# A planner that lets the parts of a dense matmul row follow each other with no latency between them

## What is computed

```python
h = rms_norm(x, norm_mix);  proj = h @ w_in               # block 0, in-projection 1024 -> 3352
o_nsa  = nsa_mixer(q, kc, vc, ks, vs, kw, vw, gates)      # 8 heads of 64
o_hgrn = hgrn2_mixer(hq, hf, hi, hg, lower_bounds, gain)  # 4 heads of 128
x = x + concat(o_nsa, o_hgrn) @ w_out
h = rms_norm(x, norm_ffn)
x = x + (silu(h @ w_gate) * (h @ w_up)) @ w_down
for l in range(2):                                        # blocks 1 and 2
    sb_q, sb_k, sb_v, df_q, df_k, df_v = split(rmsnorm(x, attn_norm[l]) @ w_in_2[l])
    mixed = concat(stick_breaking(sb_q, sb_k, sb_v), rmsnorm(differential(rope(df_q), rope(df_k), df_v)))
    x = x + mixed @ w_o[l]
    x = x + square(relu(rmsnorm(x, mlp_norm[l]) @ w_ff1[l])) @ w_ff2[l]
return rmsnorm(x, final_norm)
```

## Time and profile before

| | us |
|---|---|
| median of three timed executions | 1883.1 (1882.93 to 1883.12) |
| the profiled execution | 1884.4 |
| its span, first to last instruction | 1882.7 |
| PE busy | 1849.6 (98% of the span) |
| DVE busy | 1331.4 (71%) |
| ACT busy | 924.6 (49%) |
| POOL busy | 306.6 (16%) |

### The profile page before, as it was taken

One profiled execution on the slowest core, in us unless ns is written; L12 is line 12 of the kernel. 1 busy time (PEld: TensorE's weight loads), 2 busy tenths in 40 slices (PEclk: granted clock), 3 DMA queues, 4 the chain that ended last, 5 costly groups with the idle time before them and its releaser, 6 DMA issues.

```text
span 1882.7 us, 25125 instructions
## 1 busy us (share of the span) xinstructions
PE 1849.6 (98%) x9460; PEld 1547.3 (82%) x9460; DVE 1331.4 (71%) x2096; ACT 924.6 (49%) x1572; POOL 306.6 (16%) x378
## 2 busy tenths in 40 slices
PE   9999999999999999999999999999999999999998
PEld 7888778888888887878888888888878788888886
DVE  5476778555557877679965568787758976557886
ACT  4445776332224654457642236554547753225663
POOL 3133354000000000002412220000002322221000
PEclk9999999999999999999999999999999999999999
DMA  7222110288886662222247765563221227765664
GB/s 246 57 59 96 57 46 23 91 301 271 264 291 216 193 191 79 90 68 61 64 159 278 236 236 175 180 213 114 78 90 46 68 95 260 246 227 197 208 192 141
DMA packets 140151, 291.81 MB, mean 155 GB/s; under 512 B 12640, under 2 KB 53632, under 8 KB 140032
## 3 DMA queue, kind: packets, MB, share of 16 engines
q1 hardware_dynamic: 140032, 290.23, 46.9%
HBM read 243.00 MB, written 47.19 MB: 154 GB/s over the span
## 4 chain that ended last, share of the span: by engine, by line
PE 83%; DVE 7%; ACT 5%; POOL 2%; issue 2%; DMA 0%; POOLq 0%; SPq 0%; DVEq 0%; ACTq 0%
PE ps L49 80%; PE ps L52 3%; DVE wlo L71 2%; ACT sk1h L65 1%; POOL p L71 1%; ACT whi L65 1%; ACT p L62 1%; DVE hTl L71 1%; DVE htmp L79 1%; ACT L62 1%; DVE p L91 1%; DVE x L71 1%; ACT htmp L62 1%; POOL hTl L71 1%; DVE rot L71 0%
## 5 line engine op out<-in xcount | busy, mean ns | idle before, releaser
L65 ACT ACTIVATE whi<-raw 128x1024 fp32r<-128x1024 f32 (+1 forms) x359 | 376.0, 1051 | 480.7 <-PE ps L49 474.5
L71 DVE TENSOR_TENSOR wlo<-raw,whi 128x1024 fp32r<-128x1024 f32 (+1 forms) x359 | 442.6, 1235 | 218.4 <-ACT whi L65 214.8
L49 PE MATMUL ps<-hTh,whi 128*128 128x512 f32 (+1 forms) x1176 | 442.7, 376 | 0.0
L49 PE MATMUL ps<-hTh,wlo 128*128 128x512 f32 (+1 forms) x1176 | 438.1, 373 | 0.0
L49 PE MATMUL ps<-hTl,whi 128*128 128x512 f32 (+1 forms) x1176 | 437.9, 372 | 0.0
L49 PE MATMUL ps<-whi,hTh 128*128 128x512 f32 x934 | 374.8, 401 | 6.0 <-DVE hTl L71 3.8
L49 PE MATMUL ps<-whi,hTl 128*128 128x512 f32 x934 | 365.6, 391 | 0.0
L49 PE MATMUL ps<-wlo,hTh 128*128 128x512 f32 x934 | 365.2, 391 | 0.0
L49 PEld LDWEIGHTS ps<-hTh,wlo 128*128 128x128 f32 x1176 | 221.0, 188 | 39.5
L49 PEld LDWEIGHTS ps<-hTh,whi 128*128 128x128 f32 x1176 | 221.2, 188 | 37.0 <-DVE wlo L71 0.4
L49 PEld LDWEIGHTS ps<-hTl,whi 128*128 128x128 f32 x1176 | 221.3, 188 | 36.4
(11 more groups left out here) (260 smaller groups left out, 2470.7 us busy)
## 6 DMA issues: line engine op xcount, KB each, us to landing
raw<-in_w_ff_dram SPq DMA_DIRECT2D x96, 512.0 KB, 4.4
raw<-wsum_dram SPq DMA_DIRECT2D x64, 512.0 KB, 4.1
raw<-in_w_gate_up_dram SPq DMA_DIRECT2D x88, 256.0 KB, 4.1
wsum_dram<-htmp SPq DMA_DIRECT2D x44, 512.0 KB, 4.7
wsum_dram<-u SPq DMA_DIRECT2D x42, 512.0 KB, 5.7
raw<-in_w_in_dram SPq DMA_DIRECT2D x40, 512.0 KB, 4.6
raw<-in_w_in_dram SPq DMA_DIRECT2D x68, 256.0 KB, 3.1
u<-in_w_ff_dram SPq DMA_DIRECT2D x32, 512.0 KB, 6.1
```

The lines of the kernel that those rows point to most:

```text
L49: return self.eng.matmul(out, l, r, start=start, stop=stop, skip_group_check=True)
L65: return self.eng.activation(out, in_, ACT.Copy)
L71: return self.eng.tensor_tensor(out, a, b, op)
```

## The change

`Plan.add` notes, for a step of the sequences `gemm`, `gemm_up` and `op`, which step is before it in its sequence; `Plan.run` lets that step follow at the end of the one before, without the 0.2. Users in other sequences and on other engines still get the latency. Nothing else is changed: the same instructions are issued, with the same waits, and their order in the queues is whatever the planner now gives.

```diff
+CLOSE = ("gemm", "gemm_up", "op")
+
+
 class Plan:
     def __init__(self, T):
-        self.T, self.steps, self.rings, self.last = T, {}, {}, {}
+        self.T, self.steps, self.rings, self.last, self.behind = T, {}, {}, {}, {}
...
         if seq is not None:
             after = after + ((self.last[seq],) if seq in self.last else ())
+            self.behind[key] = self.last.get(seq) if seq in CLOSE else None
             self.last[seq] = key
...
             for u in users.get(key, ()):
                 waiting[u][0] -= 1
-                waiting[u][1] = max(waiting[u][1], end[key])
+                waiting[u][1] = max(waiting[u][1], t + dur if self.behind.get(u) == key else end[key])
```

## The result

The changed kernel takes 1889.05 us (median of six executions, 1886.9 to 1891.37) against 1883.11 for the kernel before: a ratio of 1.0027, with a 95% interval of 1.0018 to 1.0037. It is slower by some 6 us where I had forecast 4.8 us less. The profiled execution took 1890.9 us, its span is 1889.0.

A forecast was written before the change was run, and what follows sets the result against it. The bound was PE's work in sequence plus about 21 us of mixer waits. Terms: -1.9 - 1.3 - 3.2 + 1.6 = -4.8 us, so 1884.4 became 1879.6, less 1.3: 1878.3 us; 8-in-10 range 1869 to 1890.

The forecast's parts named there:

- The direct effect: On the chip the edit itself does nothing: no instruction, wait or latency removed; only the planner's clock changes.
- Term 1: Second norm's last transposes, end of each mixer: they go in after 11 to 14 half-length parts, wait gone, -1.9 us.
- Term 2: `skt` transposes after the rope, mixers 1 and 2: about half of four 0.66 us waits go, -1.3 us.
- Term 3: Waits inside the attentions and the recurrence: a quarter of 12.75 us goes, -3.2 us, bounds 0 and -12.75.
- term 4: Price of steps moved later in the stick-breaking attentions: 0.8 us in each late mixer, +1.6; mixer 0 charged nothing.
- rival (a): Waits form again elsewhere at the attentions' own pace: 1881.5 us; chance 0.30 together with the order hardly differing.
- The clock: Noted under (b): a wait over 2 us costs more than itself; mixer 0's 2.19 us wait precedes 1.2 GHz matmuls.
- (b): Slower: the attention chain becomes the bound at the ends of mixers 1 and 2, +9.3 to 1892.4 us; chance 0.16.

The follow-up runs named there:

- e7: Changed kernel with the rope of D0's tile 1 behind hTl and residual additions at lowest priority in mixers 1 and 2: 1877.14 us, ratio 0.9964.
- e1: Changed kernel, but only the in-projection's parts follow without the 0.2; out-projection and up-projection keep it: 1890.91 us, ratio 1.0037 to the kernel before.

## Why the prediction was wrong

**The direct effect and the feed-forwards: right.** The instructions on PE, DVE and POOL are the same, the feed-forwards full, mixers 1 and 2 alike in sign, though both got longer (+3.6 and +1.9) where I had each 1 to 2 us shorter.

**Term 1: right in size, -1.9, and as forecast in mixer 0 alone.** All three waits went, with no late second half behind them. But only in mixer 0 do the last transposes stand behind more half-length parts, 12; in mixers 1 and 2 they stand behind eight, where my sign was 11 to 14. There the number was luck. The last out-projection part now runs ahead of the transposes of the tile before, and the residual addition that the norm waits for follows sooner on DVE. In mixer 1 it starts 1.7 us after the start of that part's last matmul (965.03 - 963.30), where it was 4.7 (963.20 - 958.47). DVE's timelines of the kernel before and of the changed one:

```profile
963.20 0.69 DVE L71 TENSOR_TENSOR x<-ps,x 128x512 f32<-128x512 f32 x1
965.03 0.68 DVE L71 TENSOR_TENSOR x<-ps,x 128x512 f32<-128x512 f32 x1
```

**Term 2: right in mechanism, half in size.** All four waits went, -2.6 instead of -1.3.

**Term 3: this is the step that failed.** I took 1.1 us of each late mixer off as "what no order of this kind reaches", because at the first norm there is nothing else to run. No run made it clearly shorter (two waits of 0.47 to 0.59 of idle time in each late mixer of every run without the loss). That it could not become longer did not follow, and it became 2.0 us longer in each mixer. My rule for a small step that goes one part later did fit: in the changed kernel the norm's tile 2 is transposed a part later. But I let the rule decide on PE alone, where being late costs nothing as long as parts remain. The step that decided was on DVE, where the two hTl of a tile and a rope compete: in the planner's times the rope, already waiting, could start when the first hTl ended, the second hTl only DVE's own latency of 0.12 later, because only dense rows lost theirs. In the plan of before, the part ahead of that rope ended too late for this. The run with the rope moved shows it by itself: 5.1 us.

The rest of the term, with the price in term 4, has the wrong sign too. I counted -3.2 + 1.6 = -1.6; it was +3.3: +1.7 in mixer 0 and +0.8 in each late mixer. In mixer 0, where I charged no price, about 1.1 went ahead of the attention and 2.9 came beside it: the waits changed places, as rival (a) described, and those for t1l, which I had falling by a quarter, rose from 2.0 to 3.8 us of idle time. In mixers 1 and 2 the waits that the term was about (all but those at the first norm, on rot and on htmB) did fall, from 4.2 to 1.8 us of idle time and from 4.0 to 1.4, more than the quarter. The two new waits for banks brought 2.55 and 2.53 back, and behind them the clock. That was no limit of the chip's work: e7 has 1.9 and 2.1 us less waiting in the attentions than the rope run.

**Term 4: a price too small, by another mechanism.** I charged 0.8 us to each late attention, for PE steps that go a part late on their own chain. The new waits at the logits are three times that, the 2.55 and 2.53 us; that the attentions' waits grew by 0.8 in all is chance. The chain was one of banks: the transposed mix fills them, and DVE frees them behind additions, products and a scan. I had written that only `sg` and one wait on hTl are of the kind that the Trainium skill describes (Perfetto Trace Analysis, section Optimization Strategy: repeated gaps can mean that no buffer is free). In place of that wait on hTl came the two for banks, the largest of the attention. The trace agrees with the rule on the kind; it does not agree with what I drew from it, that no order would remove such a gap, since in e7 the same banks sufficed once DVE emptied them earlier.

**The clock, which was not in the sum.** I had the price in a rival and at one place, and left it out of the forecast, in which no wait grows past 2 us. So it was put at nothing. It is 3.8 of the 6.5 us in the profiled execution; by the mean clocks of the executions it is also most of the spread between them. That the clock's low stretch would grow was among the signs that I had named against me.

**The rivals.** (b) had the right sign and the wrong place: nothing at the ends of mixers 1 and 2 got longer in the changed kernel (0.2 us of idle time ahead of the second norm, before and after). Its mechanism appeared in e7, with 1.6 us a mixer, where it was outweighed, and in e1, with 1.63, 1.05 and 0.83. (a) is right for mixer 0 only. The time lies inside the range of 1869 to 1890, at the end that (b) gave it. Forecast and measured time differ by 10.8 us. In the profiled executions it is 11.3 (+6.5 against -4.8): 4.0 from the first norm, 3.8 from the clock, 4.9 on terms 3 and 4 together (I had counted -1.6, it was +3.3), less 1.3 on term 2, to 0.1. The rest is that the profiled execution of the changed kernel lies 1.8 over its median, the one before 1.3.

## What to carry to other kernels

When a planner's model changes for one engine, compare the order of every engine before pricing the change: the loss here was two places where VectorE chose between two ready steps. Price a wait of TensorE with the lower clock behind it, not by its idle time alone. A truer model is not a better plan by itself: priorities that were set under the old model may have to be set again. Here one priority and one order on VectorE were moved, and the same change went from 0.3% slower to 0.36% faster.

## What the runs showed of the hardware

A wait of 2.0 to 2.6 us on TensorE is followed by a stretch of lower clock in most cases and not in all: in the 14 profiles, behind 18 of the 23 such idle times that were not filled. The same wait of 2.02 us ahead of the logits has one behind it in mixer 1 of the changed kernel and none in mixer 2. The price is about 1.4 us at most places (some seven matmuls 0.43 us apart instead of 0.227, at a granted clock of 0.50, the 1.2 GHz level), and twice that behind one wait of the rope run. Before each such stretch in the rows above the engine had stood idle for 1.57 to 2.56 us; with matmuls without purpose in the gap none followed, in 4 of 4 places of the two profiles. The Trainium skill says something like it of a kernel that cycles through PSUM banks (TensorE: Matmul & The Clock Gate, section A second HAM failure mode: psum-queue depth-cycling): frequent short idle times between groups of matmuls bring the lower clock and cost throughput beyond themselves. The run with filled attention waits agrees on the cost, with 2.7 us; its idle times are single ones. Why the fill at the first norm gave 0.7 us and not 2.4, the attentions having two low stretches in that profile and one without it, stays open.
